# Weight units loaded in pairs, one transfer for two landing buffers

## What is computed

```python
def swiglu(h, w_in, w_out):
    gu = h @ w_in
    g, u = jnp.split(gu, 2, axis=-1)
    return (jax.nn.silu(g) * u) @ w_out
...
for layer in range(DEPTH):
    mods = jnp.split(c_silu @ ada_w[layer] + ada_b[layer], N_MOD, axis=-1)
    sh, sc, g = mods[0], mods[1], mods[2]
    h = modulate(rms_norm(x, norm_g[layer, 0]), sh, sc)
    x = x + MACARON_WEIGHT * (1.0 + g)[:, None, :] * swiglu(h, ffn_w_in[layer, 0], ffn_w_out[layer, 0])
    ...
```

## Time and profile before

| | |
|---|---|
| median of 3 runs | 1595.67 us (1594.59 to 1595.67) |
| profiled execution | 1594.07 us, of which the profile's span is 1592.3 us |
| busy, share of the span | PE 88%, DVE 79%, ACT 39%, POOL 22% |
| DMA | 308.57 MB, 194 GB/s in the mean; the queue of all loads is busy for 55.3% of the 16 DMA engines' span |
| mean granted TensorE clock | 0.940 of full speed |

### The profile page before, as it was taken

The page is one execution under the profiler, slowest core; times in us unless marked ns, Lnnn a source line. Parts: engine busy times, 40 slices in busy tenths (PEclk is TensorE's granted clock), DMA queues, the critical chain, the costliest instruction groups (busy, mean ns, idle before and its releaser), DMA issues.

```text
span 1592.3 us, 27751 instructions
## 1 busy us (share of the span) xinstructions
PE 1399.9 (88%) x10602; PEld 1319.9 (83%) x10602; DVE 1256.4 (79%) x1753; ACT 621.4 (39%) x945; POOL 344.5 (22%) x326
## 2 busy tenths in 40 slices
PE   3899997899999889999988999999979747866997
PEld 2799997899998789999877999989858636744896
DVE  6898877888777878777766887666776999999574
ACT  3333334443335343333555333345436201312343
POOL 7993000000000100000000000000630578776000
PEclk8799999999999999999989999999979878987999
DMA  9588885488873568886323888544403222212451
GB/s 375 219 304 282 296 291 210 169 307 292 303 237 119 192 231 318 295 296 225 120 80 136 293 305 297 185 153 146 159 28 106 67 68 65 80 53 79 133 177 62
DMA packets 65357, 308.57 MB, mean 194 GB/s; under 512 B 7264, under 2 KB 8576, under 8 KB 59008
## 3 DMA queue, kind: packets, MB, share of 16 engines
q1 hardware_dynamic: 65280, 307.52, 55.3%
HBM read 306.44 MB, written 1.05 MB: 193 GB/s over the span
## 4 chain that ended last, share of the span: by engine, by line
PE 67%; DVE 25%; ACT 4%; issue 3%; DMA 1%; DVEq 0%; SPq 0%; ACTq 0%
PE tiles L333 14%; PE tiles L335 13%; PE tiles L334 13%; PE acc L333 6%; PE acc L334 6%; PE acc L335 6%; DVE w_lo L325 4%; DVE arena L1614 4%; DVE arena L1220 2%; PE mods L422 2%; ACT w_hi L321 2%; PE nrm L432 1%; DVE arena L1610 1%; DVE arena L1609 1%; PE acc L575 1%
## 5 line engine op out<-in xcount | busy, mean ns | idle before, releaser
L325 DVE TENSOR_TENSOR w_lo<-land,w_hi 128x1024 fp32r<-128x1024 f32 x391 | 489.3, 1258 | 190.8 <-ACT w_hi L321 188.5
L321 ACT CAST w_hi<-land 128x1024 fp32r<-128x1024 f32 x391 | 408.3, 1046 | 574.0 <-PE tiles L335 366.0
L333 PE MATMUL tiles<-x_hi,w_hi 128*128 128x256 f32 x1464 | 421.8, 288 | 13.2 <-DVE w_lo L325 6.4
L334 PE MATMUL tiles<-x_lo,w_hi 128*128 128x256 f32 x1464 | 417.2, 285 | 0.0
L335 PE MATMUL tiles<-x_hi,w_lo 128*128 128x256 f32 x1464 | 416.9, 285 | 0.0
L333 PEld LDWEIGHTS tiles<-x_hi,w_hi 128*128 128x128 f32 x1464 | 283.5, 194 | 21.7 <-issue 13.4
L334 PEld LDWEIGHTS tiles<-x_lo,w_hi 128*128 128x128 f32 x1464 | 283.5, 194 | 1.0 <-issue 1.0
L335 PEld LDWEIGHTS tiles<-x_hi,w_lo 128*128 128x128 f32 x1464 | 283.4, 194 | 0.0
L1220 DVE SCALAR_TENSOR_TENSOR arena<-arena,csil 128x512 f32<-128x512 f32 x280 | 216.0, 771 | 2.0
L333 PE MATMUL tiles<-a_hi,w_hi 128*128 128x256 f32 (+1 forms) x656 | 191.9, 293 | 23.9 <-DVE arena L1640 20.7
L333 PE MATMUL acc<-h_hi,w_hi 128*128 128x256 f32 x704 | 202.6, 288 | 0.0
(11 more groups left out here) (302 smaller groups left out, 2043.8 us busy)
## 6 DMA issues: line engine op xcount, KB each, us to landing
land<-in_stream SPq DMA_DIRECT2D x391, 512.0 KB, 4.2
arena<-in_gstream SPq DMA_DIRECT2D x46, 2048.0 KB, 9.0
x<-in_x_t SPq DMA_DIRECT2D x1, 1024.0 KB, 14.0
arena<-in_ssm_c SPq DMA_DIRECT2D x1, 1024.0 KB, 8.0
arena<-in_ssm_b SPq DMA_DIRECT2D x1, 1024.0 KB, 4.9
out_t<-x SPq DMA_DIRECT2D x8, 128.0 KB, 1.9
cons<-in_cons SPq DMA_DIRECT2D x1, 624.5 KB, 9.0
arena<-in_band SPq DMA_DIRECT2D x1, 544.0 KB, 13.0
```

What stands on the lines that cost most here:

```text
L321: nc.scalar.copy(w_hi[:, u % RING], land[:, u % LAND]).then_inc(hi_done, 1)
L325: nc.vector.tensor_tensor(w_lo[:, u % RING], land[:, u % LAND], w_hi[:, u % RING].bitcast(F32), ALU.subtract).then_inc(lo_done, 1)
L333: nc.tensor.matmul(outs, lh, rh, start=first, stop=False, **kw)
L334: nc.tensor.matmul(outs, lh, rl, start=False, stop=False, **kw)
```

## The change

SP loads two units with one transfer of 1 MB, an even unit and the next odd one, into two adjacent landing buffers. For an odd unit `load_unit` returns at once. There are two `landed` semaphores instead of four, one for each pair of buffers. Unit 390, the last, is alone. The pair (u, u+1) waits until unit u-3 is split, since that is the later of the two whose buffers it overwrites.

```diff
-        landed = [sem(f"landed{i}") for i in range(LAND)]
+        landed = [sem(f"landed{i}") for i in range(LAND // 2)]
...
         def load_unit(sp, u, slot, i=0):
+            if u % 2:
+                return
             if u >= LAND:
-                sp.wait_ge(lo_done, i * 12 + (u - LAND + 1))
-            sp.dma_start(land[:, slot], stream[i * 12 + u]).then_inc(landed[slot], 16)
+                sp.wait_ge(lo_done, i * 12 + (u - LAND + 2))
+            n = min(2, N_UNITS - u)
+            sp.dma_start(land[:, slot:slot + n], stream[bass.ds(i * 12 + u, n)].rearrange("u p w -> p u w")
+                         ).then_inc(landed[slot // 2], 16)
 
         def split_hi(act, u, i=0):
-            act.wait_ge(landed[u % LAND], i * (16 * 12 // LAND) + 16 * (u // LAND + 1))
+            act.wait_ge(landed[u % LAND // 2], i * (16 * 12 // LAND) + 16 * (u // LAND + 1))
```

## The result

The changed kernel is slower: a median of 1606.15 us (1602.22 to 1607.79, 6 runs) against 1595.13 us for the kernel before in the same comparison (1592.94 to 1597.67, 6 runs). The ratio is 1.0064, 95% interval 1.0052 to 1.0075, so 8 to 12 us. The forecast was 1595.7; the range, 1592 to 1610, holds the result, but the likeliest case was not the one that came. The profiled execution took 1606.7 us with a span of 1604.9, which is 12.6 more than the span before.

A forecast was written before the change was run, and what follows sets the result against it. It took PE to bound the kernel (67% of the chain of waits, DVE 25%, DMA 1%). Every place was put at cost 0, so the sum was 0 and the forecast 1595.7 us, range 1592 to 1610.

The forecast's parts named there:

- The pair's price: Time from a 1 MB pair's issue to its landing: taken as 4.9 us, with 4.6 and 8.0 as the ends.
- FFN loops, cost 0: Steady state of the FFN loops: pairs and g blocks land later but in time for PE, cost 0.
- The pair behind the g block: In the FFN loops, pair (54, 55): lands at 208.3, cast at 208.91, 0.6 us spare, tightest place, twice per iteration.
- The reserve of 3.6 us: In the FFN loops, between DVE's last g-block step, ending at 226.15, and PE's reduction at 229.75.
- Rival 1: FFN loops: pair landing, two casts and a split become the bound; at 7.0 us a pair +14, 1610; chance 0.15.
- Start, cost 0: First FFN: pair (4, 5) lands at 52.8, cast at 52.95, 0.1 us spare; cost 0, up to 3.0.
- SSM entry, cost 0: Entry to SSM stage: ssm_b lands at 1230.5 behind pair (332, 333), 0.3 us spare for DVE; cost 0, up to 2.8.
- The sum, "0": Whole kernel: all places together cost 0, so the median stays at 1595.67, say 1595.7 us.
- signs that the prediction named for being wrong: PE waits on w_lo or g-block reduction every iteration, DVE waits for g blocks inside loops, or pair median over 6.5 us.
- signs for being right: 196 transfers, median 5 to 6 us; PE over 99% busy in FFNs; ACT's waits above 43 us; SSM steps near 1232.
- Rival 2: Start, SSM entry and other FFN starts give way at pairs of about 6.4 us: +5, 1601; chance 0.09.
- Rival 3: Queue: larger transfers move better, PE wins at most its 10.3 us of waits for splits, 1585.4; chance 0.05.

The follow-up runs named there:

- pairs_in_loops: Against the kernel before, only units 4 to 65 of each FFN loaded in pairs, all others one by one: 1598.33 us, ratio 1.0015.
- two_halves: The changed kernel with each pair as two back-to-back 512 KB transfers in place of one of 1 MB, ACT waiting for both: 1603.99 us, ratio 1.0053.
- the second profile: The changed kernel run once more, unchanged, for another profile: 1605.53 us, ratio 1.0065 to the kernel before, span 1601.7.
- both_landed: The kernel before, single transfers at its times, but ACT's cast of an even unit also waits for its odd partner's landing: 1641.49 us, ratio 1.0286.
- pairs_outside: Against the kernel before, units 4 to 65 of each FFN loaded one by one, all others in pairs: 1600.97 us, ratio 1.0038.
- pairs_norm_first: The changed kernel with unit 68's cast and split and g block 15's multiplication behind the norm, ssm_b ahead of pair (332, 333): 1600.37 us, ratio 1.0028.
- ssm_b_ahead: The changed kernel with ssm_b issued ahead of the pair (332, 333): 1603.28 us, ratio 1.0046 to the kernel before.
- g16_behind: The changed kernel with the pair (68, 69) issued ahead of g block 16: 1603.86 us, ratio 1.0043 to the kernel before.
- cast_after_squares: The changed kernel, same transfers, with ACT casting unit 68 behind the norm's eight squares instead of ahead: 1603.26 us, ratio 1.0042 to the kernel before.
- the two rearranged kernels: Unit 68 moved out of the norm's way in the kernel before (1595.14 us, 0.9993) and in the changed kernel with ssm_b also ahead (1600.37 us, 1.0028).

## Why the prediction was right and wrong

**The pair's price** (4.9 us, ends 4.6 and 8.0): right. The median is 5.0, and the pair (4, 5) at the start took 5.0: issued at 48.00, it was cast at 53.06. The estimate of 4.4 by the Trainium skill (DMA: Bandwidth & Descriptors, "Anatomy of one DMA"), whose fit is for transfers that GpSimd issues and not SP, was 0.6 short.

**FFN loops, cost 0**: right inside the loops, and by the reasons given; the 2.4 us of pairs_in_loops arose behind the first loop, at the norm. The pair behind the g block was the tight one. It was to have 0.6 us to spare and came 0.8 late: SP's transfers after the block, and the cast of unit 54:

```profile
202.81 11.89 SPq L319 DMA_DIRECT2D land<-in_stream  x3
```
```profile
209.75 1.05 ACT L326 CAST w_hi<-land 128x1024 fp32r<-128x1024 f32 x1 [2.61 <-DMA land<-in_stream]
```

The reserve of 3.6 us behind it was enough. Rival 1 (the landing loop, 1610) would have been near in time and is false in mechanism: the shift does not grow within an FFN, and the median pair took 5.0 us, not 6.5; those behind a g block took longer, as the 6.9 us from 202.81 to 209.75 show. Its sum was also wrong: an iteration has two g blocks and it counted one. With both it comes to 37.5 us against PE's 36.5, so it would have bound the loops at 4.9 us a pair already, which the runs refute.

**Start, cost 0**: right; 0.1 us spare was foretold, and 0.1 is what the first units shifted.

**SSM entry, cost 0**: wrong in size. The place, the queue order and the reserve of 0.3 us were right. ssm_b came about 0.5 us later than computed, and the term left out that PE's own step could take 2.08 us instead of 1.14: the granted clock over it was 0.50, before 1.00. That longer step is 0.9 of DVE's 1.30 us. The upper end of that place, 2.8, holds the measured 1.3.

**The sum, "0"**: this is the step that failed; 10 to 11 us came instead. The list "Places where order and timing are tight once" had only the places where a transfer's reader is on the path. It left out the places where ACT casts a unit that nobody needs yet, in order, ahead of work that PE does need. The row for the worst of them, a cast that already waited 3.07 us for its landing ahead of the norm's squares, was among the 21 waits and 43.2 us of the earlier trace rows; I set them aside because PE's waits for splits are small. But PE was waiting there, for the squares, and such a wait is booked to ACT L895, not to the landing. Near the end of the kernel a late landing is passed on by DVE's order. After, ACT, DVE and PE:

```profile
1540.65 1.05 ACT L326 CAST w_hi<-land 128x1024 fp32r<-128x1024 f32 x1 [2.68 <-DMA land<-in_stream]
1541.60 0.40 ACT L1186 CAST x_hi<-arena 128x256 fp32r<-128x256 f32 x1
```
```profile
1541.73 1.23 DVE L330 TENSOR_TENSOR w_lo<-land,w_hi 128x1024 fp32r<-128x1024 f32 x1 [0.27 <-ACT w_hi L326]
1542.87 0.42 DVE L1666 TENSOR_TENSOR x_lo<-arena,x_hi 128x256 fp32r<-128x256 f32 x1
```
```profile
1543.34 0.39 PE L338 MATMUL tiles<-x_hi,w_hi 128*128 128x256 f32 x1 [1.84 <-DVE x_lo L1666]
```

PE waits for `x_lo`. DVE could have made it once ACT's `x_hi` was there, but it first waits for the late cast and splits that unit. Before, the cast waited only 1.46 us, and for PE.

None of the signs that the prediction named for being wrong came: it looked for them inside the loops. One of its signs for being right did fail, as the SSM steps began at 1243.19 us and not within 1 us of 1232. And that its range reached 1606 is luck: the upper end was set by rival 1, whose mechanism did not occur.

**Rival 2** (only tight places give way, 1601) named the right mechanism, but I made it depend on pairs of 6.4 us and gave it 0.09. It needed no slower pair: pairs of 5.0 us were enough at places with no reserve at all. Its 5 us fell short by about as much again. How much of that is the clock is not measured as a whole; at the norm it is 3.0 of the 3.8 us.

**Rival 3** (larger transfers move better). The Trainium skill (DMA: Bandwidth & Descriptors, "Measured") advises transfers of 1 MiB and more. As to the queue this case agrees a little: for the same 307.5 MB, the packets took 51.8% of the 16 engines' time instead of 55.3%, and the first FFN's DMA share fell from 0.81 to 0.78. As to the time it does not: the queue was not what the kernel waited for, and two_halves, with the small transfers, is no slower than the change.

What stays open is the rest. At units 311 to 313 PE ran at a lower granted clock (0.90 from 1108.6 to 1125.5 us in the second profile, 1.00 in the same work before). DVE's splits there are no later than before, and both_landed, with single transfers throughout, has the same 0.90 (1145.0 to 1161.9 us) and the same step of 1.5 us; pairs_outside, with pairs there, has no step at unit 311, and one of 1.7 us at unit 314 of which little is left at unit 319. So pairs are not what it takes. The 0.8 us at unit 319 and the 1.5 us at unit 232 were read from traces and not tried by themselves, and pairs_norm_first still loses 4.5 us.

## What to carry to other kernels

Before a landing is made later, look not only at who needs the data but at what stands behind the wait in the program of each engine that waits: a cast or split made ahead for the next stage passes its delay on to the present one. A profile's total of waits hides this, since the loss is booked to the engine in between; follow the few waits at stage borders one by one. And when a wait is widened from one transfer to two, look what SP issues between the two.

## What the runs showed that I had not expected

In the first profile a late landing cost less by itself than by the clock that PE was granted after it: 1.2 us against 3.0 at the norm, and at unit 375 about 0.4 of the 1.8 us, where the stretch around it ran at 0.87 instead of 1.00 (before, then after):

```profile
1526.00:1538.00 12.00, 10.35 (x85) 9.94 (x84) 6.21 (x12) 5.06 (x8) 0.00 (x0) 1.00 0.47 172
```
```profile
1537.00:1550.00 13.00, 10.99 (x77) 10.59 (x76) 5.77 (x11) 4.21 (x8) 0.00 (x0) 0.87 0.44 157
```

And PE's idle time ahead does not by itself decide whether the clock falls. The 16 matmuls of the norm's sum took 5.38 us after 1.93 us of idle time, 6.71 after 2.86, 3.69 after 2.98, 6.50 after 3.16, and 3.69 after 3.71, the last in both_landed:

```profile
271.00 3.69 PE L434 MATMUL nrm<-arena,cons 128*128 128x256 f32 x16 [3.71 <-ACT arena L897]
```

Of the five profiles in which the pair (68, 69) was late at the norm, the change's two, pairs_outside, two_halves and ssm_b_ahead, the sum was slow in four and at full clock in the last. It was at full clock wherever unit 68 was out of its way (g16_behind, cast_after_squares and the two rearranged kernels). So the late landing makes the slow sum likely here, but does not decide it.

One profiled execution can thus be some 3 us off its kernel's median at such a place, and a difference of that size between two profiles is no evidence until the runs confirm it.
